# Products that nobody reads, in the last unit of each expert stage and between the router's logits and its places

## The chip, the cores and the metric

The kernel runs on one core of a Trainium2 chip. The metric is the device time of one execution in microseconds. Before the change the median of three runs is 1455.79 us (1454.13 to 1459.13). The engines are named as in the profile: PE is TensorE's matmul, PEld its weight load, DVE is VectorE, ACT is ScalarE, POOL is GpSimd, and SP is SyncE, whose queue issues the weight loads.

## What is computed

Two decoder layers over 256 tokens of width 1024, all in float32. The first mixer is a state-space scan, the second a sliding-window attention; both also attend into 256 memory tokens. Each layer ends with a mixture of experts:

```
for layer in range(2):
    h = h + mixer(layer, h, mem)
    xt = rms_norm(h)
    group = argmax(softmax(xt @ rg_w + rg_b))           # 1 of 4 groups
    e1, e2 = top2(xt @ re_w + re_b, within group)       # 2 of the 8 experts of the group
    gates = softmax(e1, e2) * group_p
    for e in range(32):
        he = silu(xt @ w_gate[e]) * (xt @ w_up[e])      # 1024 -> 512
        h = h + gates[:, e] * (he @ w_down[e])          # 512 -> 1024
return rms_norm(h)
```

The experts' weights are 6 MB each, 32 experts in each of two layers: nearly all of the 457 MB that the kernel reads.

## The kernel before

`build` runs, one after another, `mixer_a`, the expert stage of layer 0 (`moe`), `mixer_b`, the expert stage of layer 1, and `final_norm`. Each is a block in which every engine has its own instruction stream; the streams meet at the block's end and are ordered by semaphores within it. TensorE takes its stream in the order written.

**The router** (`Router`) ends each mixer. Its parts on TensorE (`Router.pe`) are transposes of the normed rows ("x2T"), the logits ("router", L483: 8 accumulating products of 36 columns for each half of the tokens), and the "places" (L489 to L493: five products of 32 columns with a triangle of ones, which count how many tokens of each expert come before each token). Between logits and places VectorE makes some 26 small instructions (`choose`, L528 to L553), each waiting for the one before, until the mask of chosen experts is there; TensorE waits for it at `pe.wait_ge(s["rt_dve"], self.MASK)` (L487). The places' bank is free by then. After the places VectorE writes counts and positions (L573, L574) and the block ends.

**The expert stage** (`Experts`) goes over 12 units (`UNITS_OF`): eight of two experts with room for 64 tokens each, then four of four experts with room for 32 tokens each. For a unit TensorE makes:

- gather (L1333): the tokens' rows picked into `xg` by products with a 0/1 matrix, in two halves; the next unit's gather is made within the unit, but the first unit's has nothing ahead of it;
- `gate_up` (L1358) for four groups in this order: gate half 0, up half 0, gate half 1, up half 1, into banks `b_gate` and `b_up`. Two or four experts use different columns of the array side by side;
- `turn_hid` (L1339), four transposes of silu(gate) * up into bank `b_turn`, which ScalarE copies out (L1304);
- `down` (L1367) for two halves, then `turn_gates` (L1344), then `scatter` (L1350): four products of 128x128 by 128x512 that add the unit's result, by token, to four banks held through the stage.

In the last unit (`last`) there is no next gather. Each group waits for its loads with `c.wait_job` (in the last unit four loads of 1 MB to a group).

**The loads.** SP issues one load of 1 MB per expert, matrix and half, in the order in which TensorE uses them, into 17 slots (`JOB_AT`). The first 17 loads of a stage are issued from within the mixer. Each further one waits until the group that used its slot before is done (`released`: `w_used` for gate and up, `down_done` for down), so the first load of the stage proper waits for the first gate group of unit 0. In layer 0 SP issues, after the last `down` group, the 11 or so loads of the second mixer; the block ends when SP is through with them. After layer 1 comes `final_norm`, which starts at the block's end.

A float32 product appears in the trace as two MATMUL records of the same shape; a scatter of four products has eight.

Of the kernel before, what the change touches and what calls it, by code (L numbers as in the profile page):

```python
# [149 lines left out]
def cut(ap, **sizes):  # L150

    (name, size), = sizes.items()
    return ap.rearrange(f"p ({name} z) -> p {name} z", **{name: size})
# [169 lines left out]
def transposes(c, pe, out, blocks, last_inc=True):  # L323

    for i, block in enumerate(blocks):
        ins = pe.transpose(out[:, i * P:(i + 1) * P], block, c.f("ident"))  # L326
    if last_inc:
        ins.then_inc(c.units_done, 1)
# [96 lines left out]
class Router:  # L425
# [44 lines left out]
    def pe(self, pe, key):  # L470
        c, U, s = self.c, self.U, self.s
        kind, i = key
        out = U.bank(key)
        if kind == "x2T":
            t, half = i // 2, i % 2
            pe.wait_ge(s["n2_dve"], 3 * t + 3)
            xs = c.xs[:, :].rearrange("q (t k p) -> q t k p", t=NT, k=KD)
            transposes(c, pe, out, [xs[:, t, 4 * half + k, :] for k in range(4)])
        elif kind == "router":
            pe.wait_ge(s["x2T_ev"], 2 * i + 2)  # L480
            pe.wait_ge(s["rw_ready"], 1)
            for k in range(KD):
                ins = pe.matmul(out[:, 0:NG + NE], cut(self.xnT, k=KD)[:, k, i * P:(i + 1) * P],  # L483
                                cut(c.f(f"route_w{self.layer}"), k=KD)[:, k, :], start=(k == 0), stop=(k == KD - 1))
            ins.then_inc(c.units_done, 1)
        else:
            pe.wait_ge(s["rt_dve"], self.MASK)  # L487
            m = cut(self.mask, t=NT)
            pe.matmul(out[:, 0:NE], c.f("tri"), m[:, 0, :], start=True, stop=True)  # L489
            pe.matmul(out[:, NE:2 * NE], c.f("ones"), m[:, 0, :], start=True, stop=False)  # L490
            pe.matmul(out[:, NE:2 * NE], c.f("tri"), m[:, 1, :], start=False, stop=True)
            pe.matmul(out[:, 2 * NE:3 * NE], c.f("ones"), m[:, 0, :], start=True, stop=False)
            pe.matmul(out[:, 2 * NE:3 * NE], c.f("ones"), m[:, 1, :], start=False, stop=True).then_inc(c.units_done, 1)  # L493
# [568 lines left out]
class Experts:  # L1062
# [87 lines left out]
    def block(self):  # L1150
        c, layer, s, o = self.c, self.layer, self.s, self.o
        jobs = expert_jobs(layer)
        with c.nc.Block() as block:
# [173 lines left out]
            def _(pe):  # L1327
                xs = c.xs[:, :].rearrange("q (t k p) -> q t k p", t=NT, k=KD)

                def gather(half, signal):  # L1330
                    for k in range(4):
                        for t in range(NT):
                            ins = pe.matmul(self.b_gather[:, k * P:(k + 1) * P], xs[:, t, 4 * half + k, :], cut(self.pick, t=NT)[:, t, :],  # L1333
                                            start=(t == 0), stop=(t == NT - 1))
                    ins.then_inc(signal, 1)

                def turn_hid(signal):
                    for j in range(4):
                        ins = pe.transpose(self.b_turn[:, j * P:(j + 1) * P], self.hid[:, j * P:(j + 1) * P], c.f("ident"))  # L1339
                    ins.then_inc(signal, 1)  # L1340

                def turn_gates(signal):
                    for t in range(NT):
                        ins = pe.transpose(self.b_turn[:, t * P:(t + 1) * P], cut(self.gated, t=NT)[:, t, :], c.f("ident"))  # L1344
                    ins.then_inc(signal, 1)

                def scatter(first, last):
                    for t in range(NT):
                        for out in range(2):
                            ins = pe.matmul(self.sums[2 * t + out][:, :], self.gates_T[:, t * P:(t + 1) * P], self.y[out][:, :],  # L1350
                                            start=first, stop=last, skip_group_check=True)
                    return ins

                def gate_up(bank, half, T, tile):
                    for k in range(4):
                        for q in range(P // T):
                            at = (4 * half + k) * P + q * T
                            ins = pe.matmul(bank[q * T:(q + 1) * T, :], self.xg[:, at:at + T], cut(tile(q), k=4)[:, k, :],  # L1358
                                            start=(half == 0 and k == 0), stop=(half == 1 and k == 3))
                    return ins  # L1360

                def down(half, T, tile):
                    for j in range(2):
                        for out in range(2):
                            for q in range(P // T):
                                at = (2 * half + j) * P + q * T
                                ins = pe.matmul(self.b_down[out][q * T:(q + 1) * T, :], self.turned[:, at:at + T],  # L1367
                                                cut(tile(q), j=2)[:, j, 512 * out:512 * out + 512],
                                                start=(half == 0 and j == 0), stop=(half == 1 and j == 1))
                    return ins  # L1370

                def side(i):
                    x = cut(c.memT1[:, :], k=KD)
                    for half in range(2):
                        c.wait_job(pe, ("mem", i, half))
                    w = lambda k: cut(c.slot(("mem", i, k // 4)), k=4)[:, k % 4, :]
                    for part in range(2):
                        bank = (self.b_gather, self.b_turn)[part]
                        if i == 0:
                            for h in range(2):  # L1380
                                at = P * (2 * part + h)
                                for k in range(KD):
                                    ins = pe.matmul(bank[:, 256 * h:256 * h + 256], w(k)[:, at:at + P], x[:, k, :], start=(k == 0), stop=(k == KD - 1))
                        else:
                            for k in range(KD):
                                ins = pe.matmul(bank[:, :], x[:, k, P * part:P * part + P], w(k), start=(k == 0), stop=(k == KD - 1))
                        ins.then_inc(s["side_done"], 1)

                def unit(u):
                    T, last = UNITS_OF[u][2], u == NU - 1  # L1390
                    if u in self.side:
                        pe.wait_ge(s["xg_ready"], u * 2 + 2)
                        side(self.side.index(u))
                    for half in range(2):
                        pe.wait_ge(s["xg_ready"], u * 2 + half + 1)
                        for what, bank in (("gate", self.b_gate), ("up", self.b_up)):
                            for q in range(P // T):
                                c.wait_job(pe, ("expert", layer, u, what, half, q))
                            gate_up(bank, half, T, lambda q: c.slot(("expert", layer, u, what, half, q))).then_inc(c.w_used, 1)
                    if u in self.side:  # L1400
                        pe.wait_ge(s["side_ev"], 2 * self.side.index(u) + 2)
                    if not last:
                        pe.wait_ge(s["pick"], u + 2)
                        gather(0, s["gathered"])
                    pe.wait_ge(s["hid_ready"], u + 1)
                    turn_hid(s["turned"])
                    for half in range(2):
                        pe.wait_ge(s["turned_ready"], u * 2 + half + 1)
                        for q in range(P // T):
                            c.wait_job(pe, ("expert", layer, u, "down", half, q))  # L1410
                        down(half, T, lambda q: c.slot(("expert", layer, u, "down", half, q))).then_inc(s["down_done"], 1)
                    pe.wait_ge(s["gated"], u + 1)
                    turn_gates(s["gates_turned"])
                    if not last:
                        pe.wait_ge(s["xg_ready"], u * 2 + 3)
                        gather(1, s["gathered"])
                    pe.wait_ge(s["y_ready"], u * 2 + 2)
                    pe.wait_ge(s["gates_ready"], u + 1)
                    ins = scatter(u == 0, last)
                    if last:  # L1420
                        ins.then_inc(s["scattered"], 1)
# [486 lines left out]
```

## Time and profile before

| | |
|---|---|
| median of three runs | 1455.79 us (1454.13 to 1459.13) |
| profiled execution | 1459.73 us |
| its span, first to last instruction | 1457.9 us |
| PE busy | 1230.5 us, 84% |
| TensorE's mean granted clock | 0.919 |
| read from memory | 456.66 MB, 314 GB/s over the span |

### The profile page before, as it was taken

Reading aid. Unit: us, or ns where it says so; the run is one execution under the profiler, and the core shown is the slowest. Engines: PE = TensorE matmul, PEld = TensorE weight load, DVE = VectorE, ACT = ScalarE, POOL = GpSimd, SP = SyncE. Lnnn points to the kernel's source line nnn. Section 1 sums busy time; section 2 is a strip of 40 time slices with the busy share of each in tenths; the row PEclk is TensorE's granted clock in tenths of the full one; section 3 lists DMA queues with packets and bytes.
Section 4 is the critical chain, followed back from the end, with each engine's and each line's share of the span. In section 5 each row is a group of like instructions: output and inputs, shape, how many; then the busy total and the mean of one; then the engine's idle time right before and its main releaser. Section 6 shows DMA issues by size and latency. Waiting matters only on the chain. (4 is left out here: it accounts for less than half of the span.)

```text
span 1457.9 us, 15099 instructions
## 1 busy us (share of the span) xinstructions
PE 1230.5 (84%) x6038; PEld 623.7 (43%) x6038; DVE 278.1 (19%) x691; ACT 199.1 (14%) x491; POOL 33.4 (2%) x42
## 2 busy tenths in 40 slices
PE   6999999889999997687643998979999999666664
PEld 6875874444443453232211466454444444222211
DVE  3542451221010100000002156022011101000001
ACT  3133231100000000000001145110000000000001
POOL 0001210000000000000000011000000000000000
PEclk9999999889999999889886999969999999778877
DMA  9534207459999999999998222538999999999994
GB/s 368 208 116 140 92 26 320 173 229 417 419 416 416 413 419 369 419 410 418 419 397 302 107 83 86 203 116 336 418 416 416 418 417 417 418 415 421 414 418 163
DMA packets 93897, 458.76 MB, mean 315 GB/s; under 512 B 7040, under 2 KB 7040, under 8 KB 60672
## 3 DMA queue, kind: packets, MB, share of 16 engines
q1 hardware_dynamic: 93824, 457.74, 78.3%
q8 instruction: 51, 0.84, 0.2%
q14 instruction: 22, 0.18, 0.0%
HBM read 456.66 MB, written 1.05 MB: 314 GB/s over the span
## 5 line engine op out<-in xcount | busy, mean ns | idle before, releaser
L1358 PE MATMUL bank<-own,e_xg 128*64 128x512 f32 (+1 forms) x1312 | 279.6, 664 | 41.4 <-DMA own<-in_w_up 18.4
L1358 PE MATMUL bank<-late,e_xg 128*64 128x512 f32 (+1 forms) x736 | 181.9, 676 | 35.6 <-DMA own<-in_w_up 19.5
L1367 PE MATMUL bank<-own,e_turned 128*32 128x512 f32 (+1 forms) x656 | 146.8, 707 | 48.2 <-DMA own<-in_w_down 34.3
L1358 PEld LDWEIGHTS bank<-own,e_xg 128*64 128x64 f32 (+1 forms) x1312 | 80.8, 134 | 199.1 <-issue 199.0
L1250 DVE TENSOR_TENSOR e_hid<-e_silu,bank 128x512 f32<-128x512 f32 x24 | 16.5, 688 | 515.0 <-ACT e_silu L1301 515.0
L1367 PE MATMUL bank<-late,e_turned 128*64 128x512 f32 (+1 forms) x368 | 91.0, 699 | 21.9 <-DMA own<-in_w_down 9.1
L1358 PEld LDWEIGHTS bank<-late,e_xg 128*64 128x64 f32 (+1 forms) x736 | 51.2, 135 | 133.8 <-issue 133.8
L1333 PE MATMUL bank<-e_pick,xs 128*128 128x128 f32 x768 | 101.1, 287 | 3.9 <-DVE e_pick L1197 2.3
L1333 PEld LDWEIGHTS bank<-e_pick,xs 128*128 128x128 f32 x768 | 94.1, 200 | 22.7 <-issue 18.0
L1367 PEld LDWEIGHTS bank<-own,e_turned 128*32 128x32 f32 (+1 forms) x656 | 41.2, 139 | 126.2 <-issue 119.5
L1301 ACT ACTIVATE e_silu<-bank 128x512 f32<-128x512 f32 x24 | 14.3, 597 | 554.9 <-PE bank L1358 554.9
L1350 PE MATMUL bank<-e_y,e_gates_T 128*128 128x512 f32 x192 | 86.5, 593 | 1.4 <-ACT e_gates_T L1309 1.4
L379 PE MATMUL bank<-a_xnT,own 128*128 128x256 f32 x384 | 85.8, 386 | 0.0
L379 PEld LDWEIGHTS bank<-a_xnT,own 128*128 128x128 f32 x384 | 74.2, 194 | 10.4
L1255 DVE COPY e_y<-bank 128x512 f32<-128x512 f32 x24 | 16.6, 692 | 263.4 <-PE bank L1367 263.4
L1367 PEld LDWEIGHTS bank<-late,e_turned 128*64 128x64 f32 (+1 forms) x368 | 25.2, 141 | 67.2 <-issue 61.5
L1350 PEld LDWEIGHTS bank<-e_y,e_gates_T 128*128 128x128 f32 x192 | 34.6, 190 | 36.3 <-issue 34.4
L1307 ACT ACTIVATE e_y<-bank 128x512 f32<-128x512 f32 x24 | 14.3, 597 | 251.8 <-PE bank L1367 251.8
L1208 DVE TENSOR_TENSOR e_xg<-bank,small 128x512 f32<-128x512 f32 x48 | 33.2, 692 | 59.6 <-PE bank L1333 59.6
L326 PE MATMUL bank<-small,xs 128*128 128x128 f32 x80 | 15.0, 359 | 32.8 <-DVE xs L407 32.8
L379 PE MATMUL bank<-own,a_xnT 128*128 128x512 f32 x96 | 42.1, 593 | 0.0
L369 PE MATMUL bank<-own,a_xbcT 128*128 128x512 f32 x96 | 41.4, 592 | 0.0
(297 smaller groups left out, 1022.6 us busy)
## 6 DMA issues: line engine op xcount, KB each, us to landing
own<-in_w_up SPq DMA_DIRECT2D x83, 1024.0 KB, 14.3
own<-in_w_down SPq DMA_DIRECT2D x82, 1024.0 KB, 15.0
own<-in_w_gate SPq DMA_DIRECT2D x81, 1024.0 KB, 15.2
late<-in_w_gate SPq DMA_DIRECT2D x47, 1024.0 KB, 16.7
late<-in_w_down SPq DMA_DIRECT2D x46, 1024.0 KB, 14.2
late<-in_w_up SPq DMA_DIRECT2D x45, 1024.0 KB, 14.4
own<-in_a_in_w SPq DMA_DIRECT2D x18, 1024.0 KB, 12.1
own<-in_mem_w_kv SPq DMA_DIRECT2D x8, 1024.0 KB, 11.2
```

Source lines behind the costliest of these rows:

```text
L326: ins = pe.transpose(out[:, i * P:(i + 1) * P], block, c.f("ident"))
L369: ins = pe.matmul(U.bank(("out", 2 * t + half))[:, :], src(4 * m + j), c.rows_at(n + m, j)[:, 512 * half:512 * half + 512], start=False, s ...
L379: ins = pe.matmul(out, lhsT(k), rhs(k), start=(k == 0), stop=(k == n - 1))
L1208: dve.tensor_tensor(cut(self.xg[:, 512 * half:512 * half + 512], k=4), cut(self.b_gather, k=4), spread_last(c.f(f"ffn_norm{layer}", 4 * ha ...
L1250: dve.tensor_tensor(self.hid[:, :], self.silu[:, :], self.b_up[:, :], ALU.mult).then_inc(s["hid_ready"], 1)
L1255: dve.tensor_copy(self.y[1][:, :], self.b_down[1][:, :]).then_inc(s["y_ready"], 1)
L1301: act.activation(self.silu[:, :], self.b_gate[:, :], ACT.Silu).then_inc(s["silu_done"], 1)
L1307: act.activation(self.y[0][:, :], self.b_down[0][:, :], ACT.Copy).then_inc(s["y_ready"], 1)
L1333: ins = pe.matmul(self.b_gather[:, k * P:(k + 1) * P], xs[:, t, 4 * half + k, :], cut(self.pick, t=NT)[:, t, :], start=(t == 0), stop=(t = ...
L1350: ins = pe.matmul(self.sums[2 * t + out][:, :], self.gates_T[:, t * P:(t + 1) * P], self.y[out][:, :], start=first, stop=last, skip_group_ ...
L1358: ins = pe.matmul(bank[q * T:(q + 1) * T, :], self.xg[:, at:at + T], cut(tile(q), k=4)[:, k, :], start=(half == 0 and k == 0), stop=(half ...
L1367: ins = pe.matmul(self.b_down[out][q * T:(q + 1) * T, :], self.turned[:, at:at + T], cut(tile(q), j=2)[:, j, 512 * out:512 * out + 512], s ...
```

## The change

Plain products of the identity with the first 512 columns of the table of constants are added to TensorE's stream. Nobody reads what they write, and the next real product into the same bank starts afresh. Four go into the places' bank, between the router's logits and the wait for the mask, in each layer. In the last unit of each expert stage five go into `b_turn` ahead of each of the waits for up half 0, gate half 1, up half 1 and down half 1 (the last after the wait for the second half of `turned`). Nothing is removed or moved, and no wait is added.

```diff
@@ Router.pe
             ins.then_inc(c.units_done, 1)
         else:
+            for _ in range(4):
+                pe.matmul(out[:, :], c.f("ident"), c.small[:, 0:512], start=True, stop=True)
             pe.wait_ge(s["rt_dve"], self.MASK)
@@ Experts, tensor stream
+                def keep_busy(n):
+                    for _ in range(n):
+                        pe.matmul(self.b_turn[:, :], c.f("ident"), c.small[:, 0:512], start=True, stop=True)
+
@@ unit(u)
                         for what, bank in (("gate", self.b_gate), ("up", self.b_up)):
+                            if last and (half, what) != (0, "gate"):
+                                keep_busy(5)
                             for q in range(P // T):
                                 c.wait_job(pe, ("expert", layer, u, what, half, q))
@@ unit(u)
                     turn_hid(s["turned"])
                     for half in range(2):
                         pe.wait_ge(s["turned_ready"], u * 2 + half + 1)
+                        if last and half == 1:
+                            keep_busy(5)
                         for q in range(P // T):
                             c.wait_job(pe, ("expert", layer, u, "down", half, q))
```

## Rows read from the trace of the kernel before

**Rows 1.** The page: clock and DMA in 40 slices of the span.

```profile
PEclk9999999889999999889886999969999999778877
DMA  9534207459999999999998222538999999999994
```

**Rows 2.** Windows (from:to, length, PE, PEld, DVE, ACT, POOL, PEclk, DMA share, GB/s): the expert stages.

```profile
320.00:340.00 20.00, 20.00 (x94) 8.05 (x92) 2.14 (x4) 0.87 (x2) 0.00 (x0) 1.00 1.02 417
...
1000.00:1420.00 420.00, 351.93 (x1913) 140.09 (x1911) 38.30 (x65) 23.04 (x55) 0.00 (x0) 0.90 1.02 417
```

**Rows 3.** Timeline (start, us, engine, line, what, [idle before]): layer 0's router, first unit.

```profile
280.38 1.95 PE L483 MATMUL bank<-small,a_xnT 128*128 128x36 f32 x16 [2.53 <-issue]
...
284.59 3.60 PE L483 MATMUL bank<-small,a_xnT 128*128 128x36 f32 x16 [0.73 <-issue]
...
293.08 0.60 PE L489 MATMUL bank<-a_acc,small 128*128 128x32 f32 x2 [4.90 <-DVE a_acc L556]
...
296.56 3.44 PE L1333 MATMUL bank<-e_pick,xs 128*128 128x128 f32 x16 [1.17 <-DVE e_pick L1197]
...
300.79 2.05 PE L1333 MATMUL bank<-e_pick,xs 128*128 128x128 f32 x16 [0.78 <-DVE e_xg L1208]
...
306.85 0.42 SPq L244 DMA_DIRECT2D own<-in_w_up  x1
```

**Rows 4.** Windows: layer 1's transposes and logits, wait for the mask, places.

```profile
962.00:965.30 3.30, 2.65 (x13) 2.24 (x12) 0.20 (x1) 1.20 (x3) 0.00 (x0) 0.50 0.51 214
965.30:969.00 3.70, 3.60 (x16) 3.49 (x16) 0.00 (x0) 1.28 (x1) 0.00 (x0) 0.50 0.00 0
969.00:973.85 4.85, 0.00 (x0) 0.00 (x0) 4.11 (x26) 0.22 (x2) 0.00 (x0) 0.50 0.00 0
973.85:977.30 3.45, 2.31 (x10) 2.21 (x10) 2.34 (x14) 0.65 (x2) 0.00 (x0) 0.50 0.00 0
```

**Rows 5.** Timeline: layer 1's two gathers.

```profile
977.36 3.78 PE L1333 MATMUL bank<-e_pick,xs 128*128 128x128 f32 x16 [1.17 <-DVE e_pick L1197]
...
981.93 3.78 PE L1333 MATMUL bank<-e_pick,xs 128*128 128x128 f32 x16 [0.78 <-DVE e_xg L1208]
```

**Rows 6.** Timeline: layer 1's last unit.

```profile
1403.91 6.06 PE L1358 MATMUL bank<-late,e_xg 128*32 128x512 f32 x32 [4.03 <-DMA late<-in_w_gate]
1404.74 0.22 PEld L1358 LDWEIGHTS bank<-late,e_xg 128*32 128x32 f32 x4 [0.62 <-issue]
1405.59 0.22 PEld L1358 LDWEIGHTS bank<-late,e_xg 128*32 128x32 f32 x4 [0.63 <-issue]
...
1424.09 3.64 PE L1367 MATMUL bank<-own,e_turned 128*32 128x512 f32 x32 [1.92 <-DMA own<-in_w_down]
...
1434.23 6.26 PE L1367 MATMUL bank<-own,e_turned 128*32 128x512 f32 x32 [6.50 <-DMA own<-in_w_down]
...
1441.57 3.67 PE L1350 MATMUL bank<-e_y,e_gates_T 128*128 128x512 f32 x8 [0.71 <-ACT e_gates_T L1309]
```

**Rows 7.** Windows of 2 us in the same unit: clock beside PE's busy time.

```profile
1408.00:1410.00 2.00, 1.97 (x16) 0.36 (x8) 0.00 (x0) 0.00 (x0) 0.00 (x0) 0.79 1.00 418
1410.00:1412.00 2.00, 0.00 (x0) 0.00 (x0) 0.00 (x0) 0.00 (x0) 0.00 (x0) 1.00 1.00 412
1412.00:1414.00 2.00, 0.12 (x4) 0.15 (x8) 0.00 (x0) 0.00 (x0) 0.00 (x0) 0.56 1.02 412
...
1422.00:1424.00 2.00, 0.17 (x2) 0.00 (x0) 0.00 (x0) 0.66 (x2) 0.00 (x0) 1.00 1.04 414
...
1432.00:1434.00 2.00, 0.00 (x0) 0.00 (x0) 0.00 (x0) 0.00 (x0) 0.00 (x0) 0.68 0.35 139
```

**Rows 8.** Timeline: layer 0's last unit, and SP's loads until the second mixer starts.

```profile
765.60 6.07 PE L1367 MATMUL bank<-late,e_turned 128*32 128x512 f32 x32 [6.52 <-DMA late<-in_w_down]
...
772.51 0.83 SPq L244 DMA_DIRECT2D own<-in_w_kv  x2
...
792.18 2.48 DVE L415 TENSOR_TENSOR h<-h,bank 128x512 f32<-128x512 f32 x4 [19.76 <-PEq L1153]
```

## The prediction

> **What bounds the kernel now.** The slices of the page come first [rows 1]. DMA is at 9 through both expert stages, so the stream of weights sets their pace; PEclk is 9 while TensorE has work without gaps and goes to 6 to 8 in the later part of each expert stage, where TensorE is faster than the loads and waits for them. The windows say the same: at 320 us and through 420 us of layer 1 the DMA share is 1.02 at 417 GB/s [rows 2]. TensorE's speed is therefore worth nothing in the middle of a stage. It counts at two ends: before the stage's own loads may start, and after the last load has landed.
>
> *The start.* The slots are full, and SP's first load waits for unit 0's first gate group. In layer 0 it is issued at 306.85 [rows 3]. Ahead of it stand the mask, the places, two gathers and that group, one behind the other, with no load running beside them (DMA share 0.00 in the three last windows of [rows 4]). TensorE waits 4.90 us for the mask [rows 3], and in that wait and around it the clock is at 0.50, 1.2 GHz [rows 4]. It is back at full only for layer 0's second gather (2.05 us against 3.44 of the first) [rows 3], and in layer 1 for neither (3.78 both) [rows 5].
>
> *The end.* In the last unit each group waits for its loads: idle 4.03 us, then 6.06 of work [rows 6]. The clock reads 1.00 just after the work, has gone to 0.56 by 1412:1414, and goes back up some 5 us into the next group, within 1408:1410 in the group of 1403.91 [rows 6, 7]. Down half 0 ran at full clock in 3.64 us, then came 6.50 idle and down half 1, mostly at half clock, in 6.26 [rows 6]; in layer 0 6.52 idle and 6.07 of work [rows 8]. After that nothing is loaded that could hide it. In layer 1 the scatter and the final norm follow. In layer 0 SP starts the next mixer's loads at 772.51, right behind down half 1, and the second mixer's first instruction at 792.18 waits for SP to be through [rows 8]; the scatter lies beside this, down half 1 does not.
>
> **What a product costs.** The scatter's four 128x128 by 128x512 products are eight records in 3.67 us [rows 6]: 0.43 per record, 0.85 per product at full clock. At half clock a record takes 0.85 (weight loads at 1404.74 and 1405.59) [rows 6], a product 1.71. So the router's four are 3.4 us at full and 6.8 at half clock, against 4.9 of idle; five in the last unit are 4.3 and 8.5, against 6.5 of idle before down half 1.
>
> **The router, part by part.** TensorE arrives at half clock. I put the rise 4.5 us after the products' start, between what the like stretches show (4.9 after 1403.91 by [rows 6, 7]; 2.9 after 296.56, where the gather's 3.44 and 2.05 show the change at about 299.5 [rows 3]). Then 2.25 us' worth of the 3.4 are done, and the rest ends 5.7 us after the logits: the places start 0.8 us later than now. Bounds: 0 if the clock rises early, 6.8 - 4.9 = 1.9 late if not at all. In return:
> - Places: ten records in the window's 2.31 us at half clock [rows 4]. At full they have no row; sixteen similar ones took 1.95 at full and 3.60 at half [rows 3], so ten take 1.2: -1.1. That is the nearest row, the bounds are 0 and that.
> - First gather: 3.44 to 2.0 in layer 0, -1.4 [rows 3]; 3.78 to 2.0 in layer 1, -1.8, and the second there -1.7 [rows 5]. This holds if the clock lasts over the 1.17 us for positions and block start. In the last unit it stayed at 1.00 through 1422:1424 with 0.17 us of work [rows 7].
> Layer 0: 0.8 - 1.1 - 1.4 = -1.7. Layer 1: 0.8 - 1.1 - 1.8 - 1.7 = -3.8. Together -5.5, and since the whole load stream starts that much earlier at an unchanged rate, it comes through. No queue is moved past: SP is already waiting for slots, VectorE's chain does not need TensorE until the places.
>
> **The last units.** Ahead of up half 0, gate half 1 and up half 1 the products fill idle time between load-bound groups (4.03 us now; 10 us per group less 3.6 at full clock leaves 6.4): worth nothing themselves. If a group and its products run over the next landing, it is by under 1 us, and SP's last loads wait for slots of gate half 0 and up half 0, some 30 us ahead of their landing. Between down half 0 and down half 1 they leave 10.14 - 3.6 - 4.3 = 2.2 us idle. A like gap, 1.92 us ahead of down half 0, did not lower the clock [rows 6, 7]. Down half 1 then takes 3.6: -2.6 in layer 1, -2.5 in layer 0. A charge stands against it. Up half 1 will end earlier at full clock, nothing is put behind it, and the wait before down half 0 grows to some 6.5 us with four transposes in it; down half 0 will often begin at half clock. With its products it is 7.7 us of full-clock work; with a rise after 4.5 us it ends 10.0 us after it began, about when the last load lands, at worst 0.7 late. I charge 0.3 for each: -4.5 for both layers. The scatter already runs at full clock.
>
> **Sum.** -5.5 - 4.5 = -10.0 us. The profiled execution took 1459.7 (span 1457.9 and 1.8 around it) and would take 1449.7; the median of the runs is 3.9 lower, and the same terms from it give 1445.8. The clock's moments differ between executions, and the median's may have been kinder, so I round to 1446.5. A measurement of this kernel can tell about 0.3%, 4.4 us, so 1451.4 is the edge of "faster".
>
> **A rule against it.** The windows of [rows 4] show TensorE busy for 2.65 of 3.30 us with transposes and logits and for 3.60 of 3.70 with logits, and the clock stays at 0.50 through the next 4.85 us. Records alone did not raise it there. The products here have the identity as one operand, as the transposes have. The Trainium skill, "TensorE: Matmul & The Clock Gate", Part 4, says that transpose-mode work does not bring the full clock because it isn't counted as busy in the same way. The new products are not in that mode, though the rule is the reason to give the rival below a chance at all.
>
> **Rivals.**
> *Not counted, and slower.* If the new products do not raise the clock, as the transposes did not, they only stand in the way. Router: 6.8 - 4.9 = 1.9 late in each layer. Last unit: down half 0 at half clock 6.9 and 8.5 of products end 15.4 after the landing, against 10.1: 5.3 late, then down half 1 at half clock; with down half 0 at full clock it is 2.0. In all 3.8 + 4 to 10.6: 1464 to 1470, taken as 1466. It decides when products fail to raise the clock within their own length. For it: the rows above. Against: 512-column float32 products are what raised it in [rows 6, 7].
> *Only the last units.* The places are small, and the clock falls again before the gathers, or the products come through late: each router gives 0.8 - 1.1 = -0.3. Sum -0.6 - 4.5: 1450.7.
> *Only the routers.* The 2.2 us of idle is enough for the clock to fall, or it falls under down half 1: -5.5 alone, 1450.3.
> *Taken up elsewhere.* The second mixer's transposes and small steps meet a worse clock: net -2, 1453.8.
>
> **Chances.** Forecast 0.62; only last units 0.14; only routers 0.08; taken up elsewhere 0.11; not counted 0.05. Forecast's own range 1441 to 1451: both router waits at their best (-1.6 in all) and no late charge give 1443, and other moments of the clock 2 more; both at their worst add 2.2 for the router and 0.8 for the tail, and places without gain 2.2. The full range adds the two half cases and most of the fourth: 1441 to 1454. Faster: 0.62 x 0.97 + about 0.12 + 0.07 = 0.79; slower 0.05; the rest, 0.16, within 0.3%.
>
> **What would show it.** Router: a group of eight records by `small` before L489, starting at the logits' end, 3.4 to 6.8 us long; places in 1.2 us, both gathers in 2.0, PEclk 1.00 from the mask on. First in_w_up load of the stage 2 and 4 us nearer to the logits. Last unit: down half 1 in 3.6 us, starting at its landing; clock 1.00 in the tail. Loads at 417 GB/s as before. It would be wrong if places start over 1.2 us late and still run 2.3, if down half 1 waits for the products rather than for its load, or if the span from first load to last landing grows.

## The result and the profile after

The changed kernel takes 1447.38 us, the median of four runs (1446.12 to 1449.15), beside 1456.73 for the kernel before (four runs, 1454.13 to 1459.13): ratio 0.9937, 95% interval 0.9915 to 0.9959. A second measurement (e5 below) gave 0.9944 (0.9922 to 0.9966). The forecast was 1446.5, with a range of 1441 to 1454.

The page of the changed kernel (clock and DMA in 40 slices, to be held against [rows 1]): counted from 0, slices 19, 20 and 38 (the last units) went from 8, 8 and 7 to 9, slices 8 and 26 (the routers) from 8 and 6 to 9 and 8, slices 16, 17 and 37 (where TensorE waits for loads) from 8 to 7, and the loads are as dense as before.

```profile
PEclk9999999899999999779997999989999999788797
DMA  9533208459999999999998312538999999999994
```

Because the stages come one after another, the span can be cut at six points and each piece compared. In both profiled executions the second half's logits of layer 0 start at the same time (284.59 and 284.61).

| piece | before | after | difference |
|---|---|---|---|
| layer 0, second logits to the stage's first in_w_up load | 22.26 | 20.24 | -2.02 |
| to SP's first load of the second mixer (in_w_kv) | 465.66 | 463.21 | -2.45 |
| to the second mixer's first instruction (DVE L415) | 19.67 | 19.41 | -0.26 |
| to layer 1's second logits | 173.20 | 171.59 | -1.61 |
| to the stage's first in_w_up load | 24.33 | 22.36 | -1.97 |
| to the final norm's first instruction | 457.13 | 455.33 | -1.80 |
| together | | | -10.1 |

The spans differ by 10.6 us (1457.9 and 1447.3); the 0.5 that is missing here lies behind the final norm's first instruction.

**Layer 0's router and first unit**, timeline of the changed kernel, answering to [rows 3]:

```profile
284.61 3.60 PE L483 MATMUL bank<-small,a_xnT 128*128 128x36 f32 x16 [0.73 <-issue]
288.02 5.58 PE L488 MATMUL bank<-small 128*128 128x512 f32 x8
...
293.44 0.30 PE L491 MATMUL bank<-a_acc,small 128*128 128x32 f32 x2
...
295.96 2.05 PE L1335 MATMUL bank<-e_pick,xs 128*128 128x128 f32 x16 [1.32 <-DVE e_pick L1199]
298.79 2.05 PE L1335 MATMUL bank<-e_pick,xs 128*128 128x128 f32 x16 [0.78 <-DVE e_xg L1210]
```

L488 is the new group: four products, eight records, 5.58 us, so it began at half clock and ended at full; the granted clock rose at 291.9, 3.9 us after the products began, and stayed at 1.00 through both gathers (windows below). The places start 8.83 us after the logits' start, against 8.49 before, so 0.34 late, and end sooner (five pairs of records 0.22 apart instead of 0.43). Both gathers take 2.05.

```profile
288.00:291.80 3.80, 3.80 (x7) 1.73 (x7) 3.03 (x18) 0.21 (x1) 0.00 (x0) 0.50 0.00 0
291.90:296.00 4.10, 2.78 (x15) 1.71 (x14) 3.27 (x21) 0.76 (x2) 0.00 (x0) 1.00 0.00 0
296.00:301.00 5.00, 4.22 (x34) 3.88 (x36) 0.81 (x2) 0.73 (x1) 0.00 (x0) 1.00 0.02 7
```

**Layer 1's router**, the same lines, answering to [rows 4, 5], then windows over the places and the first gather (columns as in [rows 2]):

```profile
959.06 3.60 PE L483 MATMUL bank<-small,b_xnT 128*128 128x36 f32 x16 [0.73 <-issue]
962.47 6.28 PE L488 MATMUL bank<-small 128*128 128x512 f32 x8
968.58 0.30 PE L491 MATMUL bank<-b_work,small 128*128 128x32 f32 x2
...
970.95 3.65 PE L1335 MATMUL bank<-e_pick,xs 128*128 128x128 f32 x16 [1.17 <-DVE e_pick L1199]
975.38 2.05 PE L1335 MATMUL bank<-e_pick,xs 128*128 128x128 f32 x16 [0.78 <-DVE e_xg L1210]
```

```profile
962.40:967.70 5.30, 5.30 (x8) 2.23 (x8) 4.26 (x26) 0.39 (x2) 0.00 (x0) 0.50 0.00 0
967.70:971.00 3.30, 2.13 (x14) 1.52 (x12) 2.19 (x13) 0.59 (x2) 0.00 (x0) 1.00 0.00 0
971.00:974.50 3.50, 3.50 (x16) 3.30 (x16) 0.00 (x0) 0.71 (x1) 0.00 (x0) 0.52 0.00 0
```

Here the clock came up only at 967.7, 5.2 us after the products began, the places started 1.0 us late at full clock, and the clock was down again for the first gather (0.52): the 3.3 us that held the end of the products, the small places and the gap behind them ended with the clock going down.

**Layer 1's last unit**, answering to [rows 6, 7]; timeline, then windows:

```profile
1399.16 4.56 PE L1378 MATMUL bank<-small 128*128 128x512 f32 x10
...
1415.80 6.54 PE L1369 MATMUL bank<-own,e_turned 128*32 128x512 f32 x32 [4.51 <-DMA own<-in_w_down]
1422.27 4.56 PE L1378 MATMUL bank<-small 128*128 128x512 f32 x10
1426.76 3.64 PE L1369 MATMUL bank<-own,e_turned 128*32 128x512 f32 x32
...
1431.48 3.67 PE L1352 MATMUL bank<-e_y,e_gates_T 128*128 128x512 f32 x8 [0.71 <-ACT e_gates_T L1311]
```

```profile
1410.00:1416.00 6.00, 0.86 (x8) 0.65 (x12) 0.58 (x1) 0.66 (x2) 0.00 (x0) 0.90 1.03 411
1416.00:1422.00 6.00, 6.00 (x32) 1.34 (x25) 0.00 (x0) 0.00 (x0) 0.00 (x0) 0.53 1.02 405
1422.00:1426.80 4.80, 4.80 (x18) 1.86 (x17) 0.00 (x0) 0.00 (x0) 0.00 (x0) 1.00 0.37 150
```

Down half 0 now runs at half clock (6.54, was 3.64): up half 1 ended early, and the clock fell in the long wait behind it; its five products bring TensorE right up to the landing and past it: down half 1 has no idle time before it. It takes 3.64 instead of 6.26, and starts 445.3 us after the stage's first in_w_up load where it was 444.5 (1434.23 less 989.71), so 0.8 us late. In layer 0 the products end 0.93 us ahead of the landing:

```profile
758.10 4.56 PE L1378 MATMUL bank<-small 128*128 128x512 f32 x10
763.59 3.64 PE L1369 MATMUL bank<-late,e_turned 128*32 128x512 f32 x32 [0.93 <-DMA late<-in_w_down]
```

### The profile page after: what moved, and what is told of

It reads as the page before. It is cut to its first block and busy times, and to the rows that moved or that the text cites. A ratio compares the mean times of both kernels' runs of the same rounds, so it can differ in the third digit from the quotient of the medians.

```text
span 1447.3 us, 15289 instructions
## 1 busy us (share of the span) xinstructions
PE 1256.7 (87%) x6134; PEld 633.6 (44%) x6134; DVE 278.1 (19%) x691; ACT 199.2 (14%) x491; POOL 33.4 (2%) x42
## 5 line engine op out<-in xcount | busy, mean ns | idle before, releaser
L1360 PE MATMUL bank<-own,e_xg 128*64 128x512 f32 (+1 forms) x1312 | 270.3, 641 | 30.1 <-DMA own<-in_w_up 15.5
L1360 PE MATMUL bank<-late,e_xg 128*64 128x512 f32 (+1 forms) x736 | 170.3, 629 | 27.6 <-DMA own<-in_w_up 12.9
L1369 PE MATMUL bank<-own,e_turned 128*32 128x512 f32 (+1 forms) x656 | 152.0, 725 | 48.5 <-DMA own<-in_w_down 32.0
L1335 PE MATMUL bank<-e_pick,xs 128*128 128x128 f32 x768 | 97.8, 281 | 4.1 <-DVE e_pick L1199 2.5
L1335 PEld LDWEIGHTS bank<-e_pick,xs 128*128 128x128 f32 x768 | 90.9, 194 | 22.8 <-issue 18.0
```

## The experiments

Ratios are to executions of the kernel before on the same chip. Its own executions scatter by 8 to 10 us (1453.6 to 1462.4 in the 31 beside e1 to e4), so a ratio of ten executions is good to 0.13 to 0.2%, 2 to 3 us. A single piece of a trace can be read to 0.01 us, but it is one execution.

| run | median us | before | ratio | 95% interval |
|---|---|---|---|---|
| e1 last units only | 1453.42 | 1457.46 | 0.9973 | 0.9959 to 0.9986 |
| e2 routers only | 1453.15 | 1457.46 | 0.9970 | 0.9951 to 0.9988 |
| e3 down half 1 only | 1456.21 | 1457.46 | 0.9989 | 0.9973 to 1.0004 |
| e4 transposes | 1456.19 | 1457.46 | 0.9983 | 0.9965 to 1.0001 |
| e5 the changed kernel | 1450.24 | 1458.44 | 0.9944 | 0.9922 to 0.9966 |
| e6 router with 8 | 1454.91 | 1458.44 | 0.9974 | 0.9954 to 0.9994 |
| e7 two ahead of the logits | 1447.47 | 1458.44 | 0.9933 | 0.9909 to 0.9957 |
| e8 all gaps filled | 1445.68 | 1458.44 | 0.9914 | 0.9895 to 0.9932 |
| e9 and 7 ahead of down half 1 | 1446.59 | 1457.82 | 0.9914 | 0.9895 to 0.9933 |
| e10 as e3 | 1459.02 | 1457.82 | 0.9996 | 0.9980 to 1.0012 |
| e11 groups only | 1457.68 | 1457.82 | 0.9997 | 0.9983 to 1.0011 |
| e12 router with 2 | 1451.82 | 1457.82 | 0.9969 | 0.9952 to 0.9986 |

### The two parts by themselves

```diff
 e1: Router.pe
-            for _ in range(4):
-                pe.matmul(out[:, :], c.f("ident"), c.small[:, 0:512], start=True, stop=True)
 e2: unit(u)
-                            if last and (half, what) != (0, "gate"):
-                                keep_busy(5)
-                        if last and half == 1:
-                            keep_busy(5)
```

> The changed kernel without the router's four products; those of the last units stay. Theory (two independent parts, each passed on in full): the first loads of the expert stages are issued as before the change (some 18.7 us after the end of the router's logits in layer 0, 20.7 in layer 1), down half 1 of both last units takes 3.6 us instead of 6.1 to 6.3. Time 1452 us (1450.5 to 1453.5), 4.5 to 5 below the kernel before. Rival (the gain is the routers' alone, the last units' is given back where down half 1 has to wait for the products): 1455 to 1457.

> The changed kernel with the router's four products alone; nothing added in the last units. Theory: the expert stage of layer 0 issues its first load about 2 us nearer to the logits' end than before, that of layer 1 2 to 4 us nearer; the load stream behind it is as long as before, and down half 1 takes some 6 us at half clock again in both layers. Time 1451.5 us (1450 to 1453). Rival (the load stream takes up the earlier start): span from first load to last landing grows by those 2 to 4 us, time 1455 to 1457.

> The changed kernel itself, for its difference with more executions: the two parts alone gave 0.27% (last units) and 0.30% (routers). Theory (they add up): ratio 0.9943, some 1449 us beside 1457.5 for the kernel before (0.992 to 0.996). Rival (they overlap, one makes the other worth less): 0.997.

Each part gives about half (0.27% and 0.30%), and together they give 0.56% to 0.63%: they add up. The medians are 1453.42 us, within what was expected of e1, and 1453.15, just above the 1450 to 1453 expected of e2. The pieces of the traces fall where the parts are. From first load to the second mixer's loads, layer 0 takes 463.3 us in e1, 465.8 in e2, 465.7 before, 463.0 in e5. From second logits to first load, layer 1 takes 22.4 in e1, 20.3 in e2, 24.3 before. In layer 0 the same piece takes 24.3 in e1, 22.4 in e2 and 22.3 before, so there e2's single profile shows no gain; the spread of this piece comes below.

Does the load stream take up an earlier start, as e2's rival says? The clearest row is layer 0 of the changed kernel: its loads start 2.02 us earlier, and down half 1, waiting for the last one, starts 458.74 us after the first (763.59 less 304.85), 458.75 before. In e2 layer 0's start was not earlier, so its 465.8 says nothing. In e2's layer 1 the loads start 4.05 us earlier and down half 1 starts 445.7 us after the first, 444.5 before: 1.1 us longer. e4 below, whose loads start only 0.4 us earlier in layer 1, has 445.9, so such a stretch comes without an early start too. So the rival, which asked for 2 to 4 us, falls. Why e2's layer 1 gave back 1.1 of its 4.05 us is not shown. e2's down half 1, at half clock as before:

```profile
763.14 6.42 PE L1369 MATMUL bank<-late,e_turned 128*32 128x512 f32 x32 [3.79 <-DMA late<-in_w_down]
...
1428.45 6.56 PE L1369 MATMUL bank<-own,e_turned 128*32 128x512 f32 x32 [3.64 <-DMA own<-in_w_down]
```

The median gain of the routers, 4.3 us, is less than the 5.5 of my sum. The traces show why. Without products the piece takes 22.3 to 25.0 us (ten values, mean 23.3: both layers of before, e1, e3, e10, e11): 22.3 to 22.6 in the six where the second gather ran at full clock, 24.3 to 25.0 in the four where neither did. With four it takes 20.2 to 22.4 (six values, mean 21.3: after, e2, e5): 20.2 to 20.3 in the three where both gathers ran at full clock, 22.3 to 22.4 in the three where the first did not. That is 2.0 per layer, 4.0 in all.

### Which of the last unit's products count

```diff
 e3, e10: Router.pe without its four products, and in unit(u)
-                            if last and (half, what) != (0, "gate"):
-                                keep_busy(5)
 e11: Router.pe without its four products, and in unit(u)
-                        if last and half == 1:
-                            keep_busy(5)
```

> The last unit's five products ahead of down half 1 alone; those ahead of up half 0, gate half 1, up half 1 and the router's are taken out. Theory (only what stands between down half 0 and down half 1 is worth anything, the other fifteen fill time that the loads set anyway): as the run with the last units' products alone, 1452 us (1450.5 to 1453.5), down half 1 in 3.6 us. Rival (the clock must be held up through the whole unit): down half 1 takes 5 us or more in at least one layer, or starts over 1 us after its landing, 1454 to 1457.

> The same kernel as e3_down_only, whose profile shows both down half 1 at 3.6 us and a span of 1449.7 while its median was only 0.11% below the kernel before. Theory (scatter of executions; what the profile shows is typical): 0.25 to 0.3% below the kernel before, as the run with all of the last unit's products. Rival (the earlier products matter: without them the clock is often low in down half 1 or the scatter): again about 0.1% below.

> The last unit's products ahead of up half 0, gate half 1 and up half 1 alone; none ahead of down half 1, none in the router. Theory (they fill time that the loads set, and 6.5 us of idle stand ahead of down half 1 as before): no gain, 0.9985 to 1.001 of the kernel before, down half 1 5 to 6.4 us. Rival (they are what makes the difference between e1_unit_only and e3_down_only): 0.2% below the kernel before.

e11 came out as expected: no gain (0.9997), down half 1 at 6.49 us in layer 0 and 4.93 in layer 1. e3 did not. Its profile and that of e10 show what I expected, down half 1 at full clock in both layers. From e10:

```profile
764.33 4.56 PE L1376 MATMUL bank<-small 128*128 128x512 f32 x10
768.82 3.64 PE L1367 MATMUL bank<-late,e_turned 128*32 128x512 f32 x32
...
1433.09 4.56 PE L1376 MATMUL bank<-small 128*128 128x512 f32 x10
1437.58 3.64 PE L1367 MATMUL bank<-own,e_turned 128*32 128x512 f32 x32
```

The stage pieces are 463.1 and 463.8 in layer 0 (465.7 before) and 455.8 in both in layer 1 (457.1 before), 3 to 4 us less in all. Yet the medians are only 0.11% and 0.04% lower, 22 executions in all. e10's executions fall into two heaps, five at 1454 to 1456 and seven at 1458 to 1461; the profiled one is of the upper. It lost its time elsewhere: 25.0 us from logits to load in layer 0, where both gathers ran at half clock, and 176.2 us in the second mixer against 173.2 before. Whether down half 1 also loses its clock in other executions is not seen in these two profiles, but e3's layer 0 shows where it could:

```profile
756.60 4.56 PE L1376 MATMUL bank<-small 128*128 128x512 f32 x10
763.21 3.64 PE L1367 MATMUL bank<-late,e_turned 128*32 128x512 f32 x32 [2.04 <-DMA late<-in_w_down]
```

Here down half 0 ran at full clock (3.64), and 2.04 us of idle were left ahead of down half 1. The clock held; in e8 below it fell behind gaps of 2.00 and 2.19 us. With the other fifteen products TensorE always stood idle 4.5 us ahead of down half 0, which then ran at half clock for most of its length, and in all twelve cases (both layers of after, e1, e5, e6, e7, e12) the gap ahead of down half 1 was 0 to 0.93 us. So the other products may count by closing this gap. That is argued: no profile of e3 or e10 shows down half 1 at half clock. The traces say that the products ahead of down half 1 suffice, the medians say that they do not, and this stays open.

### How many products, and of what kind

```diff
 e6: Router.pe (e12 the same with range(2))
-            for _ in range(4):
+            for _ in range(8):
 e4: Router.pe, and the same in keep_busy with b_turn
-                pe.matmul(out[:, :], c.f("ident"), c.small[:, 0:512], start=True, stop=True)
+                for q in range(4):
+                    pe.transpose(out[:, q * P:(q + 1) * P], c.f("ident"), c.f("ident"))
```

> Eight products instead of four between logits and places, the rest as changed. Theory: four more products at full clock are 3.4 us more work per layer in a wait that is already filled (the four ended about when the mask came), so the places start 3.4 us later than in the changed kernel, all at full clock, and both gathers surely at full clock, which gives back up to 1.7 us in one layer: 4 to 7 us slower than the changed kernel, 1452 to 1456 us. Rival (the products are free, and more of them only hold the clock better): 1446 to 1449.

> The changed kernel with two products instead of four between logits and places. Theory: at half clock they take 3.4 us, end 1.5 us before the mask, and the clock is either not up yet for the places or is down again for the gathers: gathers at half clock as in the run with transposes, first load of the stage 1 to 3 us later after the logits than in the changed kernel in each layer; 3 us slower than the changed kernel, 1452 to 1454. Rival (any products there will do): as the changed kernel, 0.9940.

> Every added product of 512 columns is replaced by four transposes of the identity of 128 columns each, which take the same time (eight records of 128 columns in 1.0 us per four transposes at full clock in the trace of before; so 0.85 us per replaced product). Theory after the Trainium skill's page on TensorE (transpose-mode work is not counted as busy and does not bring the full clock): the transposes run at half clock through the router's wait, the places start 1.9 us late in both layers at half clock, down half 1 starts 2 to 5 us late at half clock: 1464 to 1470 us. Rival (they are counted as any product of the same length): 1447 us (1445 to 1450), traces as those of the changed kernel.

Eight are too many. They take 8.84 and 8.89 us, hold the full clock over both gathers in both layers, and the piece is 23.3 and 23.4 us: as long as without any (mean 23.3), 4.7 us slower than e5 in the medians. Two are too few. In e12, layer 1, they end 1.2 us before the mask, the places run at half clock and so does the first gather:

```profile
964.84 3.76 PE L488 MATMUL bank<-small 128*128 128x512 f32 x4
969.84 0.63 PE L491 MATMUL bank<-b_work,small 128*128 128x32 f32 x2 [1.24 <-DVE b_work L555]
970.29 0.61 PE L492 MATMUL bank<-b_work,small 128*128 128x32 f32 x2
...
973.35 3.70 PE L1335 MATMUL bank<-e_pick,xs 128*128 128x128 f32 x16 [1.16 <-DVE e_pick L1199]
```

The pieces are 22.2 and 22.4, the lower end of what they are without, and the ratio is about that of e1 (0.9969, 0.9973). Of the three numbers tried four is the best.

The transposes were to test what the prediction takes from the Trainium skill, and in my expectation they were to take the products' time. They don't: a float32 transpose is one record, not two, and twenty take 2.40 us at full clock where five products take 4.56. So e4 is not a clean exchange, and its time (1456.19 us, ratio 0.9983), between the 1464 to 1470 of the theory and the 1447 of the rival, decides nothing. The clock does. Windows of e4, layer 0: the sixteen transposes, the wait behind them, places, first gather.

```profile
286.20:290.00 3.80, 3.64 (x17) 3.24 (x17) 3.04 (x18) 0.21 (x1) 0.00 (x0) 0.50 0.00 0
290.00:291.20 1.20, 0.01 (x1) 0.01 (x1) 1.05 (x7) 0.00 (x0) 0.00 (x0) 0.95 0.00 0
291.20:294.00 2.80, 1.29 (x10) 1.18 (x10) 2.20 (x15) 0.59 (x2) 0.00 (x0) 0.91 0.00 0
294.00:298.00 4.00, 3.78 (x16) 3.49 (x16) 0.13 (x2) 0.89 (x1) 0.00 (x0) 0.50 0.02 4
```

After 3.65 us of transposes the clock stands at full, and the places have it. The kernel before has the same logits ahead and nothing in the wait, and there the clock stayed at 0.50 past the places [rows 4]. So in this kernel float32 transposes raise the clock. The Trainium skill, "TensorE: Matmul & The Clock Gate", Part 4, says that the full clock does not engage for transpose-mode work; the measurement decides here. By the first gather the clock was down again (0.50). In the last unit the twenty transposes left 1.59 us of idle ahead of down half 1 in layer 0, which took 3.64, and 2.89 us in layer 1, where it took 5.34.

### Filling the other gaps

```diff
 e7, e8, e9: Router.pe, kind "router"
+            if i == 0:
+                for _ in range(2):
+                    pe.matmul(out[:, :], c.f("ident"), c.small[:, 0:512], start=True, stop=True)
             pe.wait_ge(s["x2T_ev"], 2 * i + 2)
 e8, e9: unit(u), after turn_hid
+                    if last:
+                        for _ in range(4):
+                            pe.matmul(self.b_gather[:, :], c.f("ident"), c.small[:, 0:512], start=True, stop=True)
 e8, e9: mixer_b, kind "xT", i == 0
+                        for _ in range(4):
+                            pe.matmul(c.banks[7][:, :], c.f("ident"), c.small[:, 0:512], start=True, stop=True)
                         pe.wait_ge(s["x_dve"], 6)
 e9: unit(u)
                         if last and half == 1:
-                            keep_busy(5)
+                            keep_busy(7)
```

> The changed kernel with two more products ahead of the first half's logits, in the logits' own bank, where TensorE stands idle 2.5 us at full clock just before the clock falls. Theory: the clock no longer falls before the second half's logits (1.95 us instead of 3.60), the four products run at full clock in 3.4 us, inside the 4.9 us wait: places start at once: 1.6 us and 0.5 to 1 us per layer, 4 to 5 us faster than the changed kernel, 1444 us. Rival (the clock falls anyway between the transposes and the second logits): no difference to the changed kernel, 1448 to 1449.

> The run before, and four products more after the transposes of the last unit (bank of the gathers, free there) ahead of down half 0, and four at the start of the second mixer while SP is still issuing. Theory: down half 0 runs at full clock, which is worth nothing itself, but its products end over 1 us before the last landing, 0.2 us in all; the second mixer's first transposes and products at full clock, 1 to 2 us: 1442.5 us. Rival (both fill stretches that others hide): the same as the run before.

> The run with products ahead of down half 0 and at the second mixer's start (e8_best), with seven instead of five products ahead of down half 1. In e8_best down half 0 ran at full clock (layer 1), its five products ended 2.0 and 2.2 us before the last landing, the clock fell in that idle time, and down half 1 took 5.3 us. Theory (those 2 us of idle are what cost it): seven products leave 0.3 to 0.5 us, down half 1 takes 3.6 us in both layers: 3.4 us faster than e8_best, 1442.5 us. Rival (the clock falls there because the products do not hold it, whatever their number): down half 1 over 5 us again, or late, no faster than e8_best.

The two products ahead of the logits go with a router's piece of 19.9 to 20.6 us in all six cases (e7, e8, e9, both layers); the 22.4 does not occur. The mechanism expected in e7 did not hold. Only in its layer 1 did the second logits run wholly at full clock (1.95 us; 2.99 in that of e9, 3.60 in the other four), and there the four products still took 5.38 us instead of 3.4 and the first gather 3.58. In the other five both gathers ran at full clock, against three of six without the two products; so few cases may be chance. The medians of e7 and e5 can't be told apart (1447.47, 1450.24), and the 4 to 5 us expected of e7 are not there.

e8 shows that a step of my prediction is not safe. With products ahead of it, down half 0 runs at full clock, its five products end 2.0 us before the last landing, and the clock is lost over that gap:

```profile
1416.93 4.56 PE L1381 MATMUL bank<-small 128*128 128x512 f32 x10
1423.48 5.34 PE L1372 MATMUL bank<-own,e_turned 128*32 128x512 f32 x32 [2.00 <-DMA own<-in_w_down]
```

```profile
1421.50:1423.50 2.00, 0.02 (x3) 0.05 (x4) 0.00 (x0) 0.00 (x0) 0.00 (x0) 1.00 0.28 115
1423.50:1427.00 3.50, 3.50 (x20) 1.22 (x24) 0.00 (x0) 0.00 (x0) 0.00 (x0) 0.54 0.00 0
```

The clock still reads full in the idle 2 us and falls as the real work starts, so down half 1 pays for a gap that came before it. Layer 0 shows the same (2.19 us idle, then 5.33). With seven products (e9) the gap is 0.49 us in layer 0 and 0.29 in layer 1, and down half 1 is back at 3.64:

```profile
757.04 6.28 PE L1381 MATMUL bank<-small 128*128 128x512 f32 x14
763.81 3.64 PE L1372 MATMUL bank<-late,e_turned 128*32 128x512 f32 x32 [0.49 <-DMA late<-in_w_down]
```

The stage pieces shrink from 464.8 to 463.0 and from 456.2 to 454.5, 3.4 us in all as expected, though the medians, of six executions each, show nothing of it (0.9914 both). The four products at the second mixer's start bring nothing that the traces show: from its first instruction to layer 1's second logits it takes 171.4 us in e7 without them, 171.4 and 173.7 in e8 and e9 with them. e8 and e9 both have a lower ratio than the changed kernel's 0.9937 and 0.9944, but their intervals overlap with its own, and neither reaches the 1442.5 us expected of it (1445.68, 1446.59).

## Why the prediction was right, point by point

- **What bounds the kernel**: right. Where down half 1 waited for its load, it started 458.5 to 458.8 us after the stage's first load in layer 0 and 444.4 to 445.9 in layer 1 over all the profiles, whatever TensorE's clock in between, and in layer 0 of the changed kernel the earlier start came through in full (458.74, 458.75 before).
- **Price of a product**: right in the main. From the first of five products to the next group it takes 4.49 us (1422.27 to 1426.76), against 4.3 forecast.
- **Clock's rise**: 3.9 us after the products' start in layer 0 and 5.2 in layer 1, 4.5 assumed. The places were 0.34 and 1.0 us late, 0.8 assumed.
- **Router, layer 0**: -1.7 forecast, -2.02 measured.
- **Router, layer 1**: -3.8 forecast, -1.97 measured. The step that failed is "this holds if the clock lasts over the 1.17 us for positions and block start", for which I had only the 1422:1424 window as a witness. It does not reliably last: it did in layer 0 and in e2's layer 1 (20.3 us, 4.05 less than before), but in layer 1 of the changed kernel the clock was down for the first gather. The rival "only the last units" had this mechanism, for one of the four gathers it was the true one. The size has a second fault: -3.8 was counted from one execution in which neither gather ran at full clock, which is so in four of ten pieces without products. The mean gain is 2.0 us per layer, 4.0 in all, where the sum has 5.5.
- **Last units**: -2.2 and -2.3 forecast (layers 0 and 1), -2.45 and -1.80 measured. Down half 1 took 3.64 as said, and down half 0 lost its clock as said. The charge of 0.3 for running past the landing measured 0 in layer 0 and 0.8 in layer 1. The step that 2.2 us of idle ahead of down half 1 would not lower the clock is not safe: in e8 gaps of 2.00 and 2.19 lowered it, in e3 one of 2.04 did not. Its witness, the 1.92 us ahead of down half 0, was not safe either: in e2 down half 0 took 6.39 and 6.52 us, at half clock, behind 1.75 and 1.62 us of idle. It was not put to the test in the changed kernel, since down half 0 at half clock used the gap up.
- **The products ahead of up half 0, gate half 1 and up half 1**, held to be worth nothing: by themselves they are (e11). Whether they add to those ahead of down half 1 is the open point of e3 and e10.
- **Not foreseen**: 1.61 us in the second mixer and 0.26 ahead of it. Nothing there was changed. The second mixer starts with the clock at half in both profiles; in the changed kernel it came up 9.6 us after the mixer's first instruction, before the first projection, in the kernel before 15.9 us after it, some way into it. Windows of the changed kernel over its start:

```profile
787.50:797.00 9.50, 3.16 (x15) 3.16 (x16) 6.57 (x12) 5.88 (x13) 0.67 (x1) 0.50 1.04 402
797.00:808.00 11.00, 9.21 (x24) 4.20 (x23) 2.69 (x8) 1.93 (x6) 0.00 (x0) 1.00 0.17 67
```

  This piece is 171.4 to 176.2 us long over all the profiles, so 1.6 is within what it varies by, and I don't count it to the change. Without it the sum is -8.5 us. That agrees with the ratios of 0.9937 and 0.9944, 8 to 9 us; the forecast's 10.0 was some 1.5 us too much: 1.83 in layer 1's router and 0.50 in its last unit, less 0.32 and 0.25 in layer 0 and the 0.26 ahead of the mixer. That the profiled execution came out at 1449.15 us where 1449.7 was forecast is luck in part: some 2.4 us of its gain lie in the second mixer, ahead of it and behind the final norm's first instruction.
- **The slower rival** (products not counted for the clock) is refuted by L488 alone, which would take some 7 us throughout at half clock and took 5.58 and 6.28.
- **The range**: its best case, put at 1443, works out at 1443.6 (1445.8 - 1.6 - 0.6). Nothing hangs on it.

## What to carry to other kernels

Where the loads set the pace, as in this kernel, TensorE's clock is worth money only between the last landing and the end, and ahead of the first load: fill the waits just before those two stretches, and cut the amount so that the products end with the wait. Here two brought nothing that shows and eight gave back in lateness what they won in clock (2, 4 and 8 products: 22.3, 21.3 and 23.4 us). Work out the wait at the clock that the step before it will have once the gap is filled, since a faster step ahead leaves a longer wait: idle of 2.0 and 2.2 us lost the clock in e8, and 2.0 kept it in e3, so a gap of that length is a gamble. And before a gain is counted from one profile, look how often that profile's state of the clock occurs.

## What the runs showed of the hardware

- The clock can fall after a gap is over. In e8 it read 1.00 through 2.0 us of idle and 0.54 in the 3.5 us of unbroken work behind it.
- The same gap does not always do the same: down half 1 ran at full clock behind 2.04 us of idle in e3's layer 0 and mostly at half behind 2.00 and 2.19 us in e8.
- Small products do not always keep what larger ones brought: 3.3 us that held the rest of the products, the places and the gap behind them ended with the clock down in layer 1 of the changed kernel; in its layer 0 the clock lasted through both gathers.
- Float32 transposes of the identity raised the clock after 3.65 us (e4).
- A float32 transpose of 128x128 is one record of 0.12 us at full clock, a float32 product of 128x512 two of 0.43 each.
- Executions of the kernel before differ by up to 10 us (1453.5 to 1463.3 beside e5). In the profiles, the pieces that differ without any edit in them are those in which the clock changes: 22.3 to 25.0 us around the routers without products, 171.4 to 176.2 in the second mixer. Whether the clock's moments make all of the 10 us was not tried.
